# RWKV pairs: every second unit of projection weights lowered by GpSimd in place of VectorE

## What is computed

```python
h = jnp.concatenate([x, dx], axis=-1) @ w_comb        # projections of u and its shifted difference
r, k, v, g, w_lo, a_lo = jnp.split(h, ...)            # r, k, v: 2048 wide, 32 heads of 64
w = -softplus(-(w0 + tanh(w_lo) @ w2)) - 0.5
a = sigmoid(a0 + a_lo @ a2)
kk = (k * k_k) / norm(k * k_k)
k = k * (1 + (a - 1) * k_a)
decay = exp(-exp(w))
# per head and token:  S = S * w_t + (S a_t) b_t^T + v_t k_t^T ;  y_t = S r_t
y = _wkv7_scan(r, decay, k, v, -kk, kk * a)
y = (groupnorm(y) * ln_w + ln_b + bonus) * silu(g)
return y @ w_out
```

## Time and profile before

| | |
|---|---|
| median of 3 executions | 1478.48 us (1478.38 to 1480.16) |
| the profiled execution: time / span | 1479.58 / 1477.8 us |
| PE busy / PEld busy | 1445.4 (98%) / 1318.6 (89%) us |
| DVE busy | 1024.4 us (69%), 1962 instructions |
| ACT busy | 907.4 us (61%), 2127 instructions |
| POOL busy | 59.1 us (4%), 30 instructions |
| lowerings of w_hi_rw by DVE | 126, 153.6 us, mean 1221 ns |
| lowerings by POOL | 22, 56.3 us, mean 2558 ns |

### The profile page before, as it was taken

One profiled execution on the slowest core, in us unless ns is written; L12 is line 12 of the kernel. 1 busy time (PEld: TensorE's weight loads), 2 busy tenths in 40 slices (PEclk: granted clock), 3 DMA queues, 4 the chain that ended last, 5 costly groups with the idle time before them and its releaser, 6 DMA issues.

```text
span 1477.8 us, 27893 instructions
## 1 busy us (share of the span) xinstructions
PE 1445.4 (98%) x10956; PEld 1318.6 (89%) x10956; DVE 1024.4 (69%) x1962; ACT 907.4 (61%) x2127; POOL 59.1 (4%) x30
## 2 busy tenths in 40 slices
PE   9999999999999999998999999999999999999997
PEld 8898988888999999897898989898989899799986
DVE  4468686656698875887777777777777547567764
ACT  4457667755567764476666666666666546566653
POOL 1343100000000000000000000000000000000000
PEclk9999999999999999999999999999999999999999
DMA  9464543222545555242101110111011136333340
GB/s 354 173 209 139 196 154 104 86 86 86 183 160 195 177 171 187 99 146 84 52 36 59 58 59 29 58 58 58 29 59 58 47 126 236 121 115 115 115 143 29
DMA packets 26465, 171.71 MB, mean 116 GB/s; under 512 B 3776, under 2 KB 5216, under 8 KB 6496
## 3 DMA queue, kind: packets, MB, share of 16 engines
q1 hardware_dynamic: 25152, 168.81, 32.6%
q10 hardware_dynamic: 1184, 1.11, 0.2%
HBM read 168.84 MB, written 1.08 MB: 115 GB/s over the span
## 4 chain that ended last, share of the span: by engine, by line
PE 81%; DVE 11%; ACT 6%; issue 2%; DVEq 0%; ACTq 0%
PE bank L785 10%; PE bank L786 10%; PE bank L787 9%; PE bank L1159 3%; PE bank L1328 3%; PE bank L1344 3%; PE bank L769 2%; PE bank L1160 2%; PE bank L1179 2%; PE bank L1161 2%; DVE ring L2891 2%; PE bank L967 2%; PE bank L1321 1%; DVE sd L2773 1%; PE bank L1255 1%
## 5 line engine op out<-in xcount | busy, mean ns | idle before, releaser
L685 DVE TENSOR_TENSOR ring_lo<-ring,w_hi 128x1024 fp32r<-128x1024 f32 x122 | 149.8, 1231 | 94.1 <-ACT w_hi L1601 93.1
L685 DVE TENSOR_TENSOR ring_lo<-ring,w_hi_rw 128x1024 fp32r<-128x1024 f32 x126 | 153.6, 1221 | 46.9 <-ACT w_hi_rw L1601 45.7
L1601 ACT ACTIVATE w_hi<-ring 128x1024 fp32r<-128x1024 f32 x144 | 151.9, 1057 | 29.1 <-PE bank L787 14.3
L1601 ACT ACTIVATE w_hi_rw<-ring 128x1024 fp32r<-128x1024 f32 x126 | 132.4, 1053 | 37.9 <-PE bank L1518 15.7
L1569 ACT ACTIVATE arena<-bank 128x272 f32<-128x272 f32 (+3 forms) x173 | 70.0, 406 | 110.8 <-PE bank L787 49.6
L1159 PE MATMUL bank<-x_hi,w_hi_rw 128*128 128x272 f32 x384 | 130.7, 340 | 0.9
L1160 PE MATMUL bank<-x_lo,w_hi_rw 128*128 128x272 f32 x384 | 111.0, 289 | 0.0
L1161 PE MATMUL bank<-x_hi,ring_lo 128*128 128x272 f32 x384 | 111.0, 289 | 0.0
L785 PE MATMUL bank<-u_hi,w_hi 128*128 128x256 f32 x320 | 90.0, 281 | 1.5 <-DVE ring_lo L685 1.5
L787 PE MATMUL bank<-u_hi,ring_lo 128*128 128x256 f32 x320 | 89.7, 280 | 0.0
L786 PE MATMUL bank<-u_lo,w_hi 128*128 128x256 f32 x320 | 89.6, 280 | 0.0
(11 more groups left out here) (523 smaller groups left out, 4560.2 us busy)
## 6 DMA issues: line engine op xcount, KB each, us to landing
ring<-wstream SPq DMA_DIRECT2D x151, 1024.0 KB, 4.9
arena<-spread_norms SPq DMA_DIRECT2D x1, 2048.0 KB, 7.1
con<-consts SPq DMA_DIRECT2D x1, 2024.0 KB, 13.8
h<-xT SPq DMA_DIRECT2D x1, 1024.0 KB, 6.0
sq<-spread SPq DMA_DIRECT2D x1, 1024.0 KB, 4.3
arena<-spread SPq DMA_DIRECT2D x2, 512.0 KB, 6.0
arena<-wlora ACTq DMA_DIRECT2D x1, 1024.0 KB, 9.0
out<-arena SPq DMA_DIRECT2D x4, 256.0 KB, 2.1
```

What stands on the lines that cost most here:

```text
L685: ops.tensor_tensor(lo, whole, hi.bitcast(F32), ALU.subtract).then_inc(S(signal), 1)
L1601: nc.scalar.activation(hi, whole, ACT.Copy).then_inc(S("w_hi_ready"), 1)
```

## The change

Units with an odd number from rw_pairs + 7 to rw_end - 1 (21 of the 48; rw_pairs is even) are lowered by GpSimd. `split_both` on VectorE leaves them out. GpSimd's program gets a loop behind its three memsets, which for each of these units waits until the odd units before it are done (w_lo_odd at i // 2), and then runs `split_lo`, which waits for the chunk and for the rounding. Ahead of the first odd unit of the output projection, VectorE waits until w_lo_odd has reached rw_end // 2, since from there on it raises that semaphore itself again.

```diff
+        pool_units = (rw_pairs + 6 + rw_pairs % 2, rw_pairs + 3 * PAIRS)
...
                 while both[0] < upto:
-                    split_lo(dve, V_, both[0], ("w_lo_even", "w_lo_odd")[both[0] % 2])
+                    if both[0] % 2 == 0 or not pool_units[0] <= both[0] < pool_units[1]:
+                        split_lo(dve, V_, both[0], ("w_lo_even", "w_lo_odd")[both[0] % 2])
                     both[0] += 1
...
                 while low[0] < min(upto, len(unit_start)):
+                    if low[0] == rw_end + 1:
+                        dve.wait_ge(S("w_lo_odd"), rw_end // 2)
                     split_lo(dve, V_, low[0], ("w_lo_even", "w_lo_odd")[low[0] % 2])
...
             pool.wait_ge(S("rw_zeroed"), 3)
 
+            for i in range(pool_units[0] + 1, pool_units[1], 2):
+                pool.wait_ge(S("w_lo_odd"), i // 2)
+                split_lo(pool, nc.gpsimd, i, "w_lo_odd")
+
             pool.wait_ge(S("h_tile"), 4 * DT)
```

## The result

The changed kernel takes 1483.64 us in the median (1482.12 to 1483.9, 7 executions) against 1478.82 us for the kernel before on the same chip (1478.38 to 1480.33, 7 executions). The ratio is 1.0027, with a 95% interval of 1.0017 to 1.0036: slower by 0.27%, some 4.0 us by the ratio (the two medians are 4.8 us apart). The profiled execution spans 1481.2 us, 3.4 us more than before; 1482.96 us was its time. In the code after, lines behind the first edit have moved: split_lo's instruction is L687, TensorE's lines and ScalarE's are 2 higher, VectorE's 3 or, behind split_out, 5 higher. So L2895 of before is L2900, L2888 is L2893, L2843 is L2846, L2851 is L2854, L2814 is L2817, L1222 is L1224.

A forecast was written before the change was run, and what follows sets the result against it. TensorE, busy nearly throughout, bounds the kernel; VectorE matters only at a few points. V +3.9, R -1.4 and K +0.35 sum to +2.85 us, so the median 1478.48 becomes 1481.3 us (profiled execution 1482.4); range 1476.5 to 1486.0.

The forecast's parts named there:

- V: In even pairs, GpSimd's lowering of V holds L2895, making TensorE's L1222 late by 0.60 us; sum +3.9 us.
- R: At even-to-odd pair turns, L2843 0.62 us late but mostly covered, L2888 then earlier; -0.24 us each, sum -1.4 us.
- K: In odd pairs, a held L2815 makes L2909 late, nearly covered before TensorE's L1344; 0.05 us each, sum +0.35 us.
- the first pairs: The first pair with each moved unit: V costs 0.30 us there instead of 0.60, R 0.
- The moved work: 21 lowerings go to GpSimd at 2.40 us each, 0.14 us behind the rounding; nobody waits for its result.
- VectorE's busy time: VectorE loses 25.6 us of lowerings but falls by about 10 us only, since standing still counts as busy.
- Rival 3: No cover at R and K: +10.7 us, 1489.2 us; chance 0.14; sign L1205 or L1344 waiting for VectorE every second pair.
- Rival 1: No collision that counts: V costs nothing, R gives 1.7 us, 1476.8 us; decides at lowerings under 1.7 us; chance 0.12.
- Rival 2: VectorE matters more: both waits for ScalarE (3.6 us for L2114, 2.7 for L2121) go, 1472.2 us; chance 0.05.
- Rival 4: Nothing reaches TensorE, whose rate of weight loads absorbs shifts of half a microsecond: 1478.5 us; chance 0.07.

The follow-up runs named there:

- V alone: Only the 7 V units of the odd pairs lowered by GpSimd, R and K left on VectorE, against the kernel before: 1483.24 us, ratio 1.0024.
- K alone: Only the 7 K units of the odd pairs lowered by GpSimd, against the kernel before: 1478.55 us, ratio 0.9995.
- R alone: Only the 7 R units of the even pairs lowered by GpSimd, against the kernel before: 1477.96 us, ratio 0.9990.
- the fills: The changed kernel, but GpSimd fills all 21 units' low parts with zeros in place of subtracting: 1479.00 us, ratio 0.9998.
- v_640: Only V units moved, with GpSimd subtracting 640 of 1024 columns and filling the rest with zeros: 1479.48 us, ratio 1.0001.
- R and K: The changed kernel less its V units, so 14 units on GpSimd: 1478.21 us, ratio 0.9994.
- R of all pairs: R of all pairs from 2 to 15 (14 units) on GpSimd, K and V on VectorE, against the kernel before: 1477.42 us, ratio 0.9988.
- V held back: The changed kernel, all 21 units, with GpSimd waiting ahead of V units until VectorE has masked the pair's last grams: 1478.74 us, ratio 0.9996.

## Why the prediction was right

The time lies in the range (1476.5 to 1486.0), and the forecast of +2.85 us stands against +4.0 (2.5 to 5.3). Slower by over 0.2% had 0.45 and was not the likeliest of the three, since the estimate sat on the bound; the time came out a little above it, on the side that had a little less than half the chance. The terms as the steps measure them: V +4.0, R -0.8, K 0, the first pairs -0.14, two single steps +0.41, together some 3.45 us. Point by point:

- **The moved work**: 21 at 2.38 us, 0.14 to 0.16 us behind the rounding, and nobody waits for a result of GpSimd. Right.
- **VectorE's busy time** was to fall by about 10 us and fell by 9.5.
- **V**: 0.60 us a pair, 3.9 in all. The steps are 0.62 and sum to 4.0; V alone measures +3.9. Its bounds were 0 and 2.16, and the choice of 0.60 rested on L2369 as the nearest row for L2891. The 2.48 us of L2896 under a GpSimd lowering bear that out, and the early stage was a good witness because it shows both kinds of VectorE operation beside the same GpSimd one.
- **K**: 0.05 a pair. K alone shows no difference. L2817 takes 1.20 us in place of 0.14 and its lateness is covered, as worked out. Rival 3 (no cover) is ruled out by this and by R alone. Its sign, L1205 waiting for VectorE in every second pair, did appear by name (L1207 <- L2854, 8 times), but with the same idle time: the sign was badly chosen, since only a longer wait would have meant a loss.
- **R**: this term was mis-sized. L2888 came 0.24 us earlier relative to TensorE, as worked out (0.25), but TensorE gained 0.13 us and not 0.24. The step that failed is that ScalarE's chain from L2100 to L2114 would move as one. Between them ScalarE takes a bank (L1569), and that waits for TensorE's own block. Pair 7, two lines of before and then those of after, the counterpart of the earlier trace rows:

```profile
901.18 0.42 ACT L2049 ACTIVATE ring<-sq 128x256 f32<-128x256 f32 x1
901.51 0.37 ACT L1569 ACTIVATE arena<-bank 128x272 f32<-128x272 f32 x1
...
901.87 0.24 ACT L2102 ACTIVATE u<-bank 16x16 f32<-16x16 f32 x2 [0.48 <-DVE arena L2893]
...
902.47 0.43 ACT L2051 ACTIVATE ring<-sq 128x256 f32<-128x256 f32 x1
902.86 0.40 ACT L1571 ACTIVATE arena<-bank 128x272 f32<-128x272 f32 x1
...
902.36 0.19 PEld L1163 LDWEIGHTS bank<-x_hi,ring_lo 128*128 128x128 f32 x1
...
904.34 0.11 PEld L1224 LDWEIGHTS bank<-con,arena 128*16 128x16 f32 x2
```

ScalarE's L1571 starts 0.39 us behind L2051; before, the two starts were 0.33 to 0.34 us apart. The block's last weights (L1163) are loaded at 902.36 and its product ends behind that, so the bank can't be taken much sooner. Relative to TensorE (1.53 us later here than before) L2051 is 0.24 us early, L1571 0.18 and, as it also takes 0.40 us in place of 0.37, the ScalarE instruction behind it 0.15; TensorE's L1224 is 0.12 early. The gap of 0.39 to 0.41 us stands in every odd pair from 3 on of the kernels that move R or leave it to the fills, and nowhere in the kernels that move V or K alone. That L1571 waits for the block is read from rows and not tried by a kernel of its own. Six pairs at -0.13 make -0.8 in place of -1.4.

- **The first pairs** I had set at 0 for R and K. With either moved they gave 0.1 us up to 734 us and, where V stayed, 0.2 to 0.3 more at 744 us. The first V, forecast at 0.30, cost 0.30 alone; in the changed kernel 0.28 is what a larger delay (L2900 at 1.27 in place of 1.00 us) leaves of this gain.
- **Rival 1** (no collision) is what v_640 made true: with a lowering under 1.7 us V costs nothing, the point from which it was said to decide (here 1.55). **Rival 2** (VectorE matters more) falls with the fills. **Rival 4** (TensorE absorbs half a microsecond) falls with V alone: nothing of the 0.6 us was absorbed.

**Left open.** In the changed kernel VectorE starts two instructions some 0.3 to 0.5 us late behind TensorE, though the same work went before:

```profile
796.79 0.42 DVE L2914 TENSOR_TENSOR u<-bank,con 128x256 f32<-128x256 f32 x1 [0.51 <-PE bank L1330]
...
858.87 0.42 DVE L2944 TENSOR_TENSOR sq<-sq,bank 128x256 f32<-128x256 f32 x1 [0.47 <-PE bank L1346]
```

Before, the first waited 0.16 us and the second not at all. They cost TensorE 0.10 us and, through a wait of 0.33 us at L1323, 0.31 us. This is hardly chance: the other two kernels that have all 21 units moved show both at the same places (L2914 at 796.34 and 795.27 us, L2944 at 858.09 and 857.00), and none of the other kernels does. Single steps of 0.33 us are at other places there: 975 us with K alone, 1101 with R and K, 1038 with R of all pairs; the kernel with V held back has one more at 790 us, half of which goes back. None of the runs tells why; what differs from kernel to kernel is the program, and nothing in the rows repeats with the pairs. Open too is what let the clock fall at 703 us in the profiled executions of R alone and of R and K, and in the pair stage of no other. The 0.5 us between the ratio's +4.0 and the spans' +3.4 are the noise of this account.

## What to carry to other kernels

Before giving work to an idle engine, look up in the trace which operations of the busy one stand still beside it, and then what runs at the very moment at which the moved work would start; its place decides, not its amount. Here 7 of 21 moved units made the whole loss by 0.6 us each, while a stall three times as long, behind the last consumer, cost nothing. When VectorE spends less time, ask what the next instruction on the way to TensorE waits for besides: of 25.6 us spared one at most arrived. And compare idle times, not the names of releasers; before a single step is laid on a change, look at the granted clock there.

## What the runs showed of the hardware

That VectorE's instruction with two SBUF operands stands still beside a GpSimd subtraction stands in the rows of the early stage. New to me was how exactly. Every 0.69 us instruction that met one ended 0.55 or 0.56 us after GpSimd's end, from an overlap of 0.25 us (v_640) as from one of 0.76 (867.39 + 2.39 = 869.78 against 869.02). L2846 (0.49 us alone) ends 0.29 to 0.31 us after it, and L2817, a tiny one of 128 x 2 elements, takes 1.20 us in place of 0.14. It goes both ways: GpSimd's lowering took 2.75 us in place of 2.38 where it met VectorE's L2784. A GpSimd fill (0.42 us beside L2903) holds nothing, and the maskings that read a bank take 2.48 us with and without a subtraction beside them. The Trainium skill (SBUF — State Buffer, section "Who interferes with whom") has the same three cases: two SBUF inputs against a GpSimd instruction that reads SBUF exclude each other, whichever starts first; a GpSimd instruction that only writes doesn't hold VectorE's second input; and one SBUF input is free. All three agree with the rows above.

TensorE's clock fell once for a few microseconds in the midst of busy work, with nothing in the names of the waits to show it: 0.50 between 703 and 706 us with R alone, 1.4 us lost, and 1.00 again from 707 us on.
